# Norm sums taken tile by tile on groups of 32 of TensorE's columns, and the scaling of tiles reordered, in a four-layer transformer kernel on one core

## Chip, cores and metric

The kernel runs on one core of a Trainium2 chip, in one launch. The metric is the device time of that launch in microseconds (us). Each kernel is measured several times and the median is given. One further execution is recorded by the hardware profiler; all durations of single instructions come from it. For this program a change of the time by less than about 0.2% (6.3 us) can't be told from no change.

## What is computed

Two blocks of two layers each, on 512 tokens of 1024 features, in fp32 from end to end. Cut to what matters here:

```python
def rms_norm(x, gain):
    return x * lax.rsqrt(jnp.mean(x * x, axis=-1, keepdims=True) + EPS) * gain
# first block: layer 0 mixes with HGRN2 (8 heads of 128), layer 1 with sparse attention
for layer in range(2):
    h = h + mixer(rms_norm(h, attn_norm[layer]))     # inside HGRN2: one rms norm per head
    h = h + conv_ffn(rms_norm(h, ffn_norm[layer]))   # 1024 -> 2 x 2816 -> 1024
h = rms_norm(h, final_norm)
# second block: layer 0 mixes with rotary attention (q and k normed per head), layer 1 with Hyena
for i in range(2):
    x = x + g1 * mixer(rmsnorm(x, norm1_g[i]) * (1 + sc1) + sh1)
    x = x + g2 * conv_ffn_2(rmsnorm(x, norm2_g[i]) * (1 + sc2) + sh2)
return rmsnorm(x, final_g)
```

Nine norms of the whole residual are taken this way (two of them back to back between the blocks), and each is followed by a large matrix product that needs its result.

## The kernel before

The residual `x` stays in the chip's memory transposed: eight tiles `x[:, j, :]` of 128 features (partitions) by 512 tokens. A product is made exact enough by splitting both operands into a high part in fp32r and a low part, and by three passes (lines 515, 516, 517: high with high, high with low, low with high). A weight comes in items of up to 1 MB. SyncE loads them in their order through three raw buffers, ScalarE makes the high part (`split`, line 1130) and VectorE the low part (`split_low`, line 1615). `ahead(key)` on either engine means: after the work on item `key`, split the item three further on (`NW` = 3).

The program is written by hand as one list per engine, and the engines meet at named events: `mark` raises a semaphore, `at` gives what to wait for. Nothing reorders the lists. The stages are begin, hgrn, ffn0, dsa, ffn1, attn, ffn2, hy, ffn3 and the end.

A **handover** from one stage to the next runs as follows.

- TensorE, `residual`: four items (keys 0 to 3), each giving two tiles of the new residual through `project`, which goes through the eight feature tiles and for each makes three passes for the one and three for the other column half. `project` of the next stage needs a tile of normed input per step, six passes.
- VectorE, `residual` (lines 1673, 1675): adds the two new tiles to `x`, then `ahead(keys[n])`.
- ScalarE, `residual`: squares each new tile (`squares`, line 1167), then `ahead(keys[n])`. After the last key as well: the split for a later item stands behind the last two squares and ahead of what follows.
- GpSimd, `residual` (line 2261): adds squares 0 to 5 into one buffer `rb`.
- TensorE, `token_sums` (line 558): sums over partitions by matmuls whose moving operand is one column of ones: one set (four matmuls of 128x1, in two passes each, as all fp32 matmuls here) for the buffer of the six, one for square 6, one for square 7. The result is 128 tokens (partitions) by 4 columns.
- ScalarE, `rms` (line 1138): the root. VectorE, `inverse`: reciprocal (line 1629), then a copy of each column to 128 columns (line 1631). TensorE, `spread` (line 567): four matmuls against the identity bring the factors to 128 partitions by 512 tokens in bank `STAT`.
- `shifted`: for each of the eight tiles VectorE scales (line 1642), ScalarE takes the high part (line 1145, or 1148 with a shift, in modulated stages), VectorE makes the low part (line 1646 or 1648). VectorE's list is scale 0, low 0, scale 1, low 1, and so on:

```python
dve.scalar_tensor_tensor(t[:, :], x[:, j, :], gain(j), ps[STAT][:, :], MUL, MUL)
dve.wait_ge(*at("h", stage, j, "hi"))
m = dve.tensor_tensor(hl[:, j, :], t[:, :], high, SUB)
```

The second block's stages are modulated: `modulated` first makes the gains from the conditioning. Between the blocks `end_and_modulated` does two norms in one: it sums squares and squares times the squared gain, and computes the second factor from both. The end of the kernel norms and writes out.

The same parts serve three other places. `begin` transposes the input (line 616) and sums its squares. In hgrn each of eight heads is normed over its 128 features: one set of sums, root, reciprocal, copy, spread, while other heads' projections run. In attention twelve tiles of q and k, two heads each, are normed over 64 features: there `token_sums` has two columns (`pairs`) and `spread` is in `rotate_end`. Loads of weights for gates and of the second block's `ada_w` are issued on ScalarE's queue, all others on SyncE's.

## Time and profile before

| | |
|---|---|
| median of 3 executions | 3147.76 us (3147.2 to 3148.05) |
| profiled execution, its own time | 3144.56 us |
| span of the profiled execution | 3142.8 us |
| granted clock of TensorE, mean | 0.941 of 2.4 GHz |
| TensorE busy | 2874.8 us, 91% (13568 matmuls) |
| VectorE busy | 1794.6 us, 57% (2550) |
| ScalarE busy | 1017.5 us, 32% (1366) |
| GpSimd busy | 325.4 us, 10% (271) |

The span runs from the first to the last recorded instruction. The profiled execution's own time has a little around it, and the median of the other executions is 3.2 us above that. TensorE is busy nearly always, but a share is an average: what a change at a handover is worth is read from the order of events in it. In the timeline a matmul's duration overlaps the next one's start; the pitch from start to start is what it costs in a stream. The granted clock is TensorE's alone.

### The profile page before, as it was taken

How to read it: one execution, taken by the hardware profiler on the slowest of the kernel's cores; microseconds unless marked ns; L12 is line 12 of the kernel's file. 1: busy time of each engine (PE TensorE's matmuls, PEld its weight loads, DVE VectorE, ACT ScalarE, POOL GpSimd, SP SyncE). 2: the span in 40 equal slices, each digit the busy share in tenths (PEclk: the TensorE clock that was granted, in tenths of full speed). 3: DMA queues.
4: the chain of work that ended last, by engine and by line, in shares of the span. 5: the costliest groups of instructions: out<-in, count | busy, mean ns of one | idle time of the engine just before them, and what ended most of it. 6: DMA issues, size and time to landing. Idle time of an engine off the chain costs nothing.

```text
span 3142.8 us, 33865 instructions
## 1 busy us (share of the span) xinstructions
PE 2874.8 (91%) x13568; PEld 2308.3 (73%) x13568; DVE 1794.6 (57%) x2550; ACT 1017.5 (32%) x1366; POOL 325.4 (10%) x271
## 2 busy tenths in 40 slices
PE   7988789999997799999997789999998988899999
PEld 6777678888774478888783367888777777678887
DVE  3277746565576437474545536564655798554433
ACT  3223224242333434242424423232332233332322
POOL 0000000000001200000202310000000677200000
PEclk9999889999997899999898989999999688999999
DMA  5710114443322024343320015454421000322221
GB/s 141 154 41 27 41 54 144 134 133 112 89 67 68 21 77 141 121 141 97 102 67 14 1 54 163 155 174 133 140 81 44 26 18 22 111 78 94 95 86 47
DMA packets 260436, 275.67 MB, mean 88 GB/s; under 512 B 23159, under 2 KB 229495, under 8 KB 260280
## 3 DMA queue, kind: packets, MB, share of 16 engines
q1 hardware_dynamic: 230088, 218.44, 22.8%
q10 hardware_dynamic: 30192, 55.05, 5.6%
q8 instruction: 109, 1.79, 0.3%
q14 instruction: 47, 0.39, 0.0%
HBM read 266.13 MB, written 7.34 MB: 87 GB/s over the span
## 4 chain that ended last, share of the span: by engine, by line
PE 75%; DVE 14%; ACT 5%; issue 3%; DMA 1%; SPq 1%; POOL 0%; ACTq 0%; DVEq 0%; POOLq 0%
PE ps L515 21%; PE ps L517 21%; PE ps L516 21%; DVE sb L1615 2%; PE ps L800 2%; DVE sb L1642 2%; PE ps L665 1%; PE ps L558 1%; DMA sb<-in_hgrn_w_in 1%; PE ps L567 1%; PE ps L783 1%; PE ps L979 1%; ACT sb L1456 1%; DVE sb L2023 1%; DVE sb L2156 1%
## 5 line engine op out<-in xcount | busy, mean ns | idle before, releaser
L515 PE MATMUL ps<-sb 128*128 128x512 f32 (+1 forms) x3552 | 1364.6, 384 | 93.2 <-DVE sb L1648 18.8
L516 PE MATMUL ps<-sb 128*128 128x512 f32 (+1 forms) x3552 | 1347.4, 379 | 0.0
L517 PE MATMUL ps<-sb 128*128 128x512 f32 (+1 forms) x3552 | 1347.3, 379 | 0.0
L515 PEld LDWEIGHTS ps<-sb 128*128 128x128 f32 x3552 | 687.4, 194 | 248.6 <-issue 68.5
L517 PEld LDWEIGHTS ps<-sb 128*128 128x128 f32 x3552 | 687.1, 193 | 125.0
L516 PEld LDWEIGHTS ps<-sb 128*128 128x128 f32 x3552 | 688.1, 194 | 119.1 <-issue 0.7
L1615 DVE TENSOR_TENSOR sb<-sb 128x2048 fp32r<-128x2048 f32 (+2 forms) x198 | 446.6, 2256 | 372.2 <-ACT sb L1130 372.1
L1130 ACT ACTIVATE sb<-sb 128x2048 fp32r<-128x2048 f32 (+2 forms) x198 | 368.7, 1862 | 291.2 <-PE ps L517 272.5
L1800 DVE SCALAR_TENSOR_TENSOR sb<-ps,sb 128x511 f32<-128x511 f32 (+1 forms) x264 | 197.7, 749 | 190.2 <-ACT sb L1288 184.0
L2261 POOL TENSOR_TENSOR sb<-sb 128x512 f32<-128x512 f32 x45 | 62.1, 1387 | 1714.0 <-ACT sb L1167 1712.0
L1288 ACT ACTIVATE sb<-ps,sb 128x512 f32<-128x512 f32 x132 | 100.1, 774 | 304.9 <-PE ps L517 304.9
L783 PE MATMUL ps<-sb 128*128 128x128 f32 x416 | 75.7, 326 | 65.4 <-ACT sb L1342 62.2
L1675 DVE SCALAR_TENSOR_TENSOR sb<-ps,sb 128x512 f32<-128x512 f32 x64 | 46.3, 751 | 153.8 <-PE ps L517 153.6
L1820 DVE SCALAR_TENSOR_TENSOR sb<-sb 128x512 f32<-128x512 f32 x168 | 126.0, 750 | 12.9 <-DVE sb L1817 0.5
L783 PEld LDWEIGHTS ps<-sb 128*128 128x128 f32 x416 | 56.4, 167 | 102.7 <-issue 96.8
L2293 POOL TENSOR_SCALAR sb<-sb 128x512 f32<-128x512 f32 (+3 forms) x128 | 76.7, 612 | 485.7 <-DVE sb L1877 485.7
L1673 DVE TENSOR_TENSOR sb<-sb,ps 128x512 f32<-128x512 f32 x64 | 43.5, 687 | 127.4 <-PE ps L517 127.2
L1315 ACT ACTIVATE sb<-sb 128x512 fp32r<-128x512 f32 x88 | 55.3, 633 | 180.1 <-DVE sb L1842 108.5
L1167 ACT ACTIVATE sb<-sb 128x512 f32<-128x512 f32 x72 | 45.0, 642 | 206.0 <-DVE sb L1675 108.9
L1300 ACT ACTIVATE sb<-sb 128x512 f32<-128x512 f32 x88 | 55.6, 632 | 137.1 <-DVE sb L1800 137.1
L665 PEld LDWEIGHTS ps<-sb 128*128 128x128 f32 x512 | 72.6, 210 | 28.9 <-issue 23.6
L665 PE MATMUL ps<-sb 128*128 128x128 f32 x512 | 75.2, 295 | 18.8 <-DVE sb L1721 18.8
(213 smaller groups left out, 2354.2 us busy)
## 6 DMA issues: line engine op xcount, KB each, us to landing
sb<-in_ffn_w_up SPq DMA_DIRECT2D x88, 1024.0 KB, 5.1
sb<-in_ada_w ACTq DMA_DIRECT2D x192, 256.0 KB, 3.2
sb<-in_ffn_w_down SPq DMA_DIRECT2D x32, 1024.0 KB, 5.0
sb<-in_ffn_w_down SPq DMA_DIRECT2D x16, 768.0 KB, 4.3
sb<-in_hy_w_in SPq DMA_DIRECT2D x12, 1024.0 KB, 5.1
sb<-in_hgrn_w_in SPq DMA_DIRECT2D x8, 1024.0 KB, 11.1
sb<-in_hgrn_w_in SPq DMA_DIRECT2D x16, 512.0 KB, 5.5
sb<-in_dsa_w_in SPq DMA_DIRECT2D x6, 1024.0 KB, 5.3
```

The source lines that it names most:

```text
L515: pe.matmul(o, al, bh, start=f, stop=False, **kw)
L516: pe.matmul(o, ah, bl, start=False, stop=False, **kw)
L517: m = pe.matmul(o, ah, bh, start=False, stop=l, **kw)
L665: m = pe.matmul(ps[bk][:, c], a_[:, c], b_[:, c], start=True, stop=True)
L783: m = pe.transpose(ps[b][:, c], M.P[2 * (u % 4) + e][:, c], ident[:, :])
L800: m = pe.matmul(ps[b][64 * e:64 * e + 64, q0:L], value(j, s), M.PT[e][:, s, q0:L], start=s == 0, stop=s == 3, skip_group_check=True)
L1130: act.activation(wh[w][:, 0:n], raw[it["r"]][:, 0:n], ACTF.Copy).then_inc(*mark("act_hi", ("hi", it["key"])))
L1288: act.activation(dst[:, :], ps[b][:, :], ACTF.Identity, bias=bias(tile), scale=wt(offset, tile)).then_inc(*mark("act_ffn", (name + "_0", n ...
L1615: dve.tensor_tensor(wl[w][:, 0:n], raw[it["r"]][:, 0:n], wh[w][:, 0:n].bitcast(F), SUB).then_inc(*mark("dve_lo", ("lo", it["key"])))
L1800: dve.scalar_tensor_tensor(o, i, cv[0](tap, tile), o, MUL, ADD).then_inc(*mark("dve_ffn", (name, n, tile) if last else (name + "_1", n, ti ...
L1820: m = dve.scalar_tensor_tensor(a, w[:, :], cact[:, f:f + 1], a, MUL, ADD)
L2293: pool.tensor_scalar(P, P, M.rs[:, c:c + 1], 1.0, MUL, MUL).then_inc(*mark(f"pool_{stage}", ("scaled", stage, u, e)))
```

## The change

**Sums.** `sums` takes the place of `token_sums`. For each quarter `tt` of the tokens a matmul has 32 columns of ones as weights, the 128 columns of squares as the moving operand, and writes to partitions 32 tt to 32 tt + 31 of the bank: each quarter has its own group of 32 of TensorE's columns. The sum of a token thus stands on 32 partitions. Every tile of squares has its own set now: eight sets a norm (sixteen in the double norm, whose second kind goes to bank `OTHER`). Two sets stand behind key 1, two behind key 2, two between the column halves of key 3 (`project` has an argument `cols`), and two at the end. GpSimd's additions are gone.

**Factor.** `rms` and `inverse` work on 128 columns (256 in attention) in `rb`; the copy is gone; the double norm's steps are widened alike. `spread` multiplies, for each quarter, 32 partitions of the factor with ones: the 32 equal rows are summed, and `eps` and the scale carry 1024 to make up for it. Each of the four matmuls waits for the one before (`("spread", *name, tt - 1)`). `begin`, the heads and the rotary part use the same functions or the same form.

**Tiles.** VectorE's list in `shifted` is scale 0, scale 1, low 0, scale 2, low 1, and so on.

**Weights.** After the last key of a residual, `ahead` stands on ScalarE and VectorE no longer in `residual` but behind `shifted` of the next stage (argument `then`).

```diff
-STAT, OB, HB = 7, 3, 7
+STAT, OTHER, OB, HB = 7, 3, 3, 7
...
-    def project(sem, key, banks, done, then, tile=None, ready=None, rows=None):
+    def project(sem, key, banks, done, then, tile=None, ready=None, rows=None, cols=(0, 1)):
...
-    def token_sums(bank, src, cols, first, last, to=0):
-        n = cols.shape[1]
+    def sums(bank, squares, first, last):
         for tt in range(4):
-            m = pe.matmul(ps[bank][:, to + n * tt:to + n * tt + n], src[:, 128 * tt:128 * tt + 128], cols,
-                          start=first and tt == 0, stop=last, skip_group_check=True)
+            m = pe.matmul(ps[bank][32 * tt:32 * tt + 32, 0:128], ones[:, 0:32], squares[:, 128 * tt:128 * tt + 128],
+                          start=first, stop=last, skip_group_check=True)
         return m
-    def spread(bank, i, scaled, done):
-        pe.wait_ge(*at(*scaled))
-        wait_bank(bank)
+    def spread(bank, i, name):
+        pe.wait_ge(*at("inverse", *name))
         for tt in range(4):
-            m = pe.matmul(ps[bank][:, 128 * tt:128 * tt + 128], rb[i][:, 128 * tt:128 * tt + 128], ident[:, :],
-                          start=True, stop=True, skip_group_check=True)
-        m.then_inc(*mark("pe_stat", done))
+            p = slice(32 * tt, 32 * tt + 32)
+            if tt:
+                pe.wait_ge(*at("spread", *name, tt - 1))
+            pe.matmul(ps[bank][:, 128 * tt:128 * tt + 128], ones[p, :], rb[i][p, 0:128], start=True, stop=True,
+                      skip_group_check=True).then_inc(*mark("pe_stat", ("spread", *name, tt), *([("spread", *name)] if tt == 3 else [])))
     def normalise(stage, i):
-        freed[STAT] = [("rms", stage)]
-        spread(STAT, i, ("wide", stage), ("spread", stage))
+        spread(STAT, i, (stage,))
         freed[STAT] = [("t", stage, 7)]
     def residual(sem, r, keys, banks, ready, tile=None, stats=True, gain=False):
+        def squared(j):
+            for i in ((0, 1) if gain else (0,)):
+                if j == 0:
+                    wait_bank((STAT, OTHER)[i])
+                pe.wait_ge(*at("sq", r, i, j))
+                sums((STAT, OTHER)[i], (ht if i else sq)[j % 2], j == 0, j == NT - 1).then_inc(
+                    *mark("pe_stat", ("sq_used", r, i, j), *([("stat", r, i)] if j == NT - 1 else [])))
         for n in range(4):
-            bk = banks[n % 2]
-            project(sem, keys[n], bk, [("res", r, 2 * n + i) for i in range(2)],
-                    [[("x", r, 2 * n + i)] for i in range(2)], tile=tile, ready=ready)
+            names = [("res", r, 2 * n + i) for i in range(2)]
+            then = [[("x", r, 2 * n + i)] for i in range(2)]
+            if stats and n == 3:
+                project(sem, keys[n], banks[n % 2], names, then, tile=tile, ready=ready, cols=(0,))
+                squared(4)
+                squared(5)
+                project(sem, keys[n], banks[n % 2], names, then, tile=tile, ready=ready, cols=(1,))
+            else:
+                project(sem, keys[n], banks[n % 2], names, then, tile=tile, ready=ready)
+                if stats and n:
+                    squared(2 * n - 2)
+                    squared(2 * n - 1)
         if stats:
-            kinds = (0, 1) if gain else (0,)
-            for i in kinds:
-                if i == 0:
-                    wait_bank(STAT)
-                pe.wait_ge(*at("sum", r, i, 5))
-                token_sums(STAT, rb[i], ones[:, 0:1], i == 0, False, to=4 * i)
-                pe.wait_ge(*at("sq", r, i, 6))
-                token_sums(STAT, (ht if i else sq)[0], ones[:, 0:1], False, False, to=4 * i).then_inc(
-                    *mark("pe_stat", ("sq_used", r, i, 6)))
-            for i in kinds:
-                pe.wait_ge(*at("sq", r, i, 7))
-                token_sums(STAT, (ht if i else sq)[1], ones[:, 0:1], False, True, to=4 * i).then_inc(
-                    *mark("pe_stat", ("sq_used", r, i, 7), *([("stat", r)] if i == kinds[-1] else [])))
+            squared(6)
+            squared(7)
...
-            token_sums(b1, sq[n % 2], T.pairs[:, :], True, True).then_inc(*mark("pe_attn", ("rot_sum", n)))
-            freed[b1] = [("rms", "rot", n)]
+            for e in range(2):
+                for half in range(2):
+                    p = 64 * e + 32 * half
+                    m = pe.matmul(ps[b1][p:p + 32, 0:256], ones[64 * e:64 * e + 64, 0:32], sq[n % 2][64 * e:64 * e + 64, 256 * half:256 * half + 256],
+                                  start=True, stop=True, skip_group_check=True)
+            m.then_inc(*mark("pe_attn", ("rot_sum", n)))
...
         def rotate_end(n):
             b1 = ((4, 5), (6, 7))[n % 2][0]
-            spread(b1, n % 2, ("wide", "rot", n), ("spread", "rot", n))
+            pe.wait_ge(*at("inverse", "rot", n))
+            for half in range(2):
+                if half:
+                    pe.wait_ge(*at("spread", "rot", n, 0))
+                for e in range(2):
+                    p = slice(64 * e + 32 * half, 64 * e + 32 * half + 32)
+                    m = pe.matmul(ps[b1][64 * e:64 * e + 64, 256 * half:256 * half + 256], ones[p, 0:64], rb[n % 2][p, 0:256],
+                                  start=True, stop=True, skip_group_check=True)
+                m.then_inc(*mark("pe_stat", ("spread", "rot", n, half), *([("spread", "rot", n)] if half else [])))
...
-    def rms(i, heads, bank, n, done, name):
-        w = 4 * heads
+    def rms(i, bank, n, done, name, width=128):
         act.wait_ge(*at(*done))
-        act.activation(rc[i][:, 0:w], ps[bank][:, 0:w], ACTF.Sqrt, bias=eps[:, 0:1], scale=1.0 / n).then_inc(*mark("act_stat", name))
-    def shifted(stage, shift):
+        act.activation(rb[i][:, 0:width], ps[bank][:, 0:width], ACTF.Sqrt, bias=eps[:, 0:1], scale=1024.0 / n).then_inc(
+            *mark("act_stat", ("rms", *name)))
+    def shifted(stage, shift, then=None):
         for j in range(NT):
...
-    def normalise(stage, i, r, shift=None):
-        rms(i, 1, STAT, D, ("stat", r), ("rms", stage))
-        shifted(stage, shift)
+        if then:
+            ahead(then)
+    def normalise(stage, i, r, then, shift=None):
+        rms(i, STAT, D, ("stat", r, 0), (stage,))
+        shifted(stage, shift, then)
...
-            if j == 0:
-                dst = rb[i]
-            else:
-                dst = (ht if i else sq)[j % 2]
-                if j >= 3:
-                    act.wait_ge(*at("sum", r, i, j - 2))
+            dst = (ht if i else sq)[j % 2]
+            if j >= 2:
+                act.wait_ge(*at("sq_used", r, i, j - 2))
...
                 squares(r, 2 * n + 1, gain)
-            ahead(keys[n])
+            if n < 3 or not stats:
+                ahead(keys[n])
...
-    def inverse(i, heads, rooted, wide):
-        w = 4 * heads
-        dve.wait_ge(*at(*rooted))
-        dve.reciprocal(rc[i][:, 0:w], rc[i][:, 0:w]).then_inc(*step("inverse", wide))
-        dve.wait_ge(*at("inverse", wide))
-        dve.tensor_copy(rb[i][:, :].rearrange("p (c f) -> p c f", c=w),
-                        rc[i][:, 0:w].unsqueeze(2).broadcast_to([128, w, 128 // heads])).then_inc(*mark("dve_stat", wide))
-    def shifted(stage, r, gain, shift, within=None):
+    def inverse(i, name, width=128):
+        dve.wait_ge(*at("rms", *name))
+        dve.reciprocal(rb[i][:, 0:width], rb[i][:, 0:width]).then_inc(*mark("dve_stat", ("inverse", *name)))
+    def shifted(stage, r, gain, shift, then=None, within=None):
         dve.wait_ge(*at("spread", stage))
-        for j in range(NT):
-            t = ht[j % 2]
-            dve.wait_ge(*at("x", r, j))
-            if j >= 2:
-                dve.wait_ge(*at("h", stage, j - 2, "hi"))
-                dve.wait_ge(*at("h", stage, j - 2, "lo"))
-            dve.scalar_tensor_tensor(t[:, :], x[:, j, :], gain(j), ps[STAT][:, :], MUL, MUL).then_inc(*mark("dve_h", ("t", stage, j)))
-            dve.wait_ge(*at("h", stage, j, "hi"))
-            high = hh[:, j, :].bitcast(F)
-            if shift is None:
-                m = dve.tensor_tensor(hl[:, j, :], t[:, :], high, SUB)
-            else:
-                m = dve.scalar_tensor_tensor(hl[:, j, :], t[:, :], mod[:, shift + j:shift + j + 1], high, ADD, SUB)
-            m.then_inc(*mark("dve_h", ("h", stage, j, "lo")))
-            if j == 1 and within:
-                within()
-    def normalise(stage, i, r, gain, shift=None, within=None):
-        inverse(i, 1, ("rms", stage), ("wide", stage))
-        shifted(stage, r, gain, shift, within)
-    def modulated(stage, i, r, layer, gain, first):
+        for j in range(NT + 1):
+            if j < NT:
+                dve.wait_ge(*at("x", r, j))
+                if j >= 2:
+                    dve.wait_ge(*at("h", stage, j - 2, "lo"))
+                dve.scalar_tensor_tensor(ht[j % 2][:, :], x[:, j, :], gain(j), ps[STAT][:, :], MUL, MUL).then_inc(*mark("dve_h", ("t", stage, j)))
+            if j:
+                k = j - 1
+                dve.wait_ge(*at("h", stage, k, "hi"))
+                t, high = ht[k % 2], hh[:, k, :].bitcast(F)
+                if shift is None:
+                    m = dve.tensor_tensor(hl[:, k, :], t[:, :], high, SUB)
+                else:
+                    m = dve.scalar_tensor_tensor(hl[:, k, :], t[:, :], mod[:, shift + k:shift + k + 1], high, ADD, SUB)
+                m.then_inc(*mark("dve_h", ("h", stage, k, "lo")))
+                if k == 1 and within:
+                    within()
+        if then:
+            ahead(then)
+    def normalise(stage, i, r, gain, shift=None, then=None, within=None):
+        inverse(i, (stage,))
+        shifted(stage, r, gain, shift, then, within)
...
-            ahead(keys[n])
+            if n < 3 or not stats:
+                ahead(keys[n])
...
-    def residual(r, gain=False):
-        for j in range(1, NT - 2):
-            for i in ((0, 1) if gain else (0,)):
-                pool.wait_ge(*at("sq", r, i, j))
-                pool.wait_ge(*(at("sum", r, i, j - 1) if j > 1 else at("sq", r, i, 0)))
-                pool.tensor_tensor(rb[i][:, :], rb[i][:, :], (ht if i else sq)[j % 2][:, :], ADD).then_inc(
-                    *mark("pool_sum", ("sum", r, i, j)))
     def begin():
         pool.memset(ones[:, :], 1.0).then_inc(*mark("pool_begin", ("ones",)))
-        pool.memset(eps[:, :], EPS).then_inc(*mark("pool_begin", ("eps",)))
+        pool.memset(eps[:, :], 1024 * EPS).then_inc(*mark("pool_begin", ("eps",)))
...
-    normalise("ffn0", 1, 1, lambda j: v("ffn_norm", j))
+    normalise("ffn0", 1, 1, lambda j: v("ffn_norm", j), None, ("hgrn", "out", 3))
...
```

In the list of TensorE, at the end of the residual of hgrn and the start of ffn0's first product, there stood (behind the name of a semaphore is who is waited for: `act_sq` is ScalarE's squares, `act_stat` and `dve_stat` the factor's steps):

```order
L558 MATMUL ps<-sb 128x1 [waits pool_sum,dve_hgrn]
L558 MATMUL ps<-sb 128x1 x3
L558 MATMUL ps<-sb 128x1 [waits act_sq]
L558 MATMUL ps<-sb 128x1 x3
L558 MATMUL ps<-sb 128x1 [waits act_sq]
L558 MATMUL ps<-sb 128x1 x3
L567 MATMUL ps<-sb 128x128 [waits act_stat,dve_stat]
L567 MATMUL ps<-sb 128x128 x3
L515 MATMUL ps<-sb 128x512 [waits act_h,dve_h,dve_lo,act_hi]
```

and now stand:

```order
L514 MATMUL ps<-sb 128x512
L556 MATMUL ps<-sb 32x128 [waits act_sq]
L556 MATMUL ps<-sb 32x128 x3
L556 MATMUL ps<-sb 32x128 [waits act_sq]
L556 MATMUL ps<-sb 32x128 x3
L567 MATMUL ps<-sb 128x128 [waits dve_stat]
L567 MATMUL ps<-sb 128x128 [waits pe_stat] x3
L512 MATMUL ps<-sb 128x512 [waits act_h,dve_h,dve_lo,act_hi]
```

Two sets are left here instead of three, the other six stand in three pairs farther up among the products, and the spreading matmuls wait for each other.

In the list of VectorE, at the same place (`act_h` is the high part of a tile, `dve_x` the residual), there stood:

```order
L1673 TENSOR_TENSOR sb<-sb,ps 128x512 [waits pe_hgrn] x2
L1615 TENSOR_TENSOR sb<-sb 128x2048 [waits act_hi]
L1629 RECIPROCAL sb<-sb 128x4 [waits act_stat]
L1631 COPY sb<-sb 128x512 [waits dve_step]
L1642 SCALAR_TENSOR_TENSOR sb<-sb,ps 128x512 [waits dve_x,pe_stat]
L1646 TENSOR_TENSOR sb<-sb 128x512 [waits act_h]
L1642 SCALAR_TENSOR_TENSOR sb<-sb,ps 128x512 [waits dve_x]
L1646 TENSOR_TENSOR sb<-sb 128x512 [waits act_h]
L1642 SCALAR_TENSOR_TENSOR sb<-sb,ps 128x512 [waits dve_h,dve_x]
```

and now stand:

```order
L1685 TENSOR_TENSOR sb<-sb,ps 128x512 [waits pe_hgrn] x2
L1641 RECIPROCAL sb<-sb 128x128 [waits act_stat]
L1650 SCALAR_TENSOR_TENSOR sb<-sb,ps 128x512 [waits dve_x,pe_stat]
L1650 SCALAR_TENSOR_TENSOR sb<-sb,ps 128x512 [waits dve_x]
L1656 TENSOR_TENSOR sb<-sb 128x512 [waits act_h]
L1650 SCALAR_TENSOR_TENSOR sb<-sb,ps 128x512 [waits dve_h,dve_x]
L1656 TENSOR_TENSOR sb<-sb 128x512 [waits act_h]
L1650 SCALAR_TENSOR_TENSOR sb<-sb,ps 128x512 [waits dve_h,dve_x]
```

The weight's low part (128x2048) and the copy have left the way to the first scaling, and the second scaling has passed the first low part.

## Rows read from the trace of the kernel before

**Rows 1.** The chain of waits that ended last, share of the span by engine
```profile
PE 75%; DVE 14%; ACT 5%; issue 3%; DMA 1%; SPq 1%; POOL 0%; ACTq 0%; DVEq 0%; POOLq 0%
```
**Rows 2.** Timeline, TensorE, into ffn0: start, us, line, shape, count [idle before, releaser]
```profile
446.61 2.92 PE L558 MATMUL ps<-sb 128*128 128x1 f32 x24
452.89 2.07 PE L567 MATMUL ps<-sb 128*128 128x128 f32 x8 [3.36 <-DVE sb L1631]
457.29 0.77 PE L515 MATMUL ps<-sb 128*128 128x512 f32 x1 [2.32 <-DVE sb L1646]
...
471.63 0.47 PE L515 MATMUL ps<-sb 128*128 128x512 f32 x1 [0.42 <-DVE sb L1646]
```
**Rows 3.** The same view, VectorE
```profile
450.00 2.29 DVE L1615 TENSOR_TENSOR sb<-sb 128x2048 fp32r<-128x2048 f32 x1 [2.50 <-ACT sb L1130]
452.21 0.17 DVE L1629 RECIPROCAL sb<-sb 128x4 f32<-128x4 f32 x1
...
455.00 0.75 DVE L1642 SCALAR_TENSOR_TENSOR sb<-sb,ps 128x512 f32<-128x512 f32 x1 [2.17 <-PE ps L567]
456.45 0.69 DVE L1646 TENSOR_TENSOR sb<-sb 128x512 fp32r<-128x512 f32 x1 [0.70 <-ACT sb L1145]
457.06 0.74 DVE L1642 SCALAR_TENSOR_TENSOR sb<-sb,ps 128x512 f32<-128x512 f32 x1
```
**Rows 4.** The same view, ScalarE
```profile
446.85 1.32 ACT L1167 ACTIVATE sb<-sb 128x512 f32<-128x512 f32 x2 [7.76 <-DVE sb L1673]
448.07 1.89 ACT L1130 ACTIVATE sb<-sb 128x2048 fp32r<-128x2048 f32 x1
449.87 0.24 ACT L1138 ACTIVATE sb<-ps,sb 128x4 f32<-128x4 f32 x1
```
**Rows 5.** Windows: us, busy of PE, PEld, DVE, ACT, POOL, PEclk, DMA share, GB/s
```profile
450.00:453.00 3.00, 0.11 (x1) 0.11 (x1) 2.80 (x3) 0.12 (x1) 0.00 (x0) 0.50 0.00 0
463.00:466.00 3.00, 3.00 (x14) 2.33 (x13) 2.30 (x4) 0.63 (x1) 0.00 (x0) 1.00 0.01 3
```
**Rows 6.** Timeline, TensorE in attention: two groups of 64 columns, and rows halved
```profile
1733.86 0.65 PE L800 MATMUL ps<-sb 128*64 128x512 f32 x2
...
1734.34 0.60 PE L800 MATMUL ps<-sb 128*64 128x512 f32 x2
...
998.26 0.49 PE L868 MATMUL ps<-sb 64*128 64x128 f32 x4
998.68 0.44 PE L873 MATMUL ps<-sb 128*128 128x128 f32 x2
```
**Rows 7.** Timeline, TensorE in hgrn: sums and spread of a head
```profile
283.87 0.95 PE L558 MATMUL ps<-sb 128*128 128x1 f32 x8
...
265.12 1.06 PE L567 MATMUL ps<-sb 128*128 128x128 f32 x8
```
**Rows 8.** Groups by line and form, VectorE: count, busy us, mean ns, idle before
```profile
L1877 DVE RECIPROCAL sb<-sb 128x2 f32<-128x2 f32 x64 | 10.5, 164 | 71.1 <-ACT sb L1456 39.6 <-ACT sb L1405 31.5
...
L1629 DVE RECIPROCAL sb<-sb 128x8 f32<-128x8 f32 x12 | 2.4, 200 | 9.7 <-ACT sb L1138 9.7
```
**Rows 9.** Timeline, TensorE, spread of the norm into dsa
```profile
834.07 1.26 PE L567 MATMUL ps<-sb 128*128 128x128 f32 x8 [0.82 <-DVE sb L1631]
```
**Rows 10.** Timeline, VectorE, scalings of a modulated norm (into attention)
```profile
1543.35 0.74 DVE L1642 SCALAR_TENSOR_TENSOR sb<-sb,ps 128x512 f32<-128x512 f32 x1
...
1545.55 0.74 DVE L1642 SCALAR_TENSOR_TENSOR sb<-sb,ps 128x512 f32<-128x512 f32 x1
```
**Rows 11.** The chain in order of time, first 135 us: start, us, what
```profile
27.19 3.33 PE ps L558 x16
...
33.65 0.76 DVE sb L1642
...
53.43 2.30 DVE sb L1615
...
77.27 39.04 DMA sb<-in_hgrn_w_in
```

More of the change, by code:

```diff
@@ L1578, in act_program @@
             hgrn()
[L1579 removed]
+            normalise("ffn0", 1, 1, ("hgrn", "out", 3))
             ffn(0, "hgrn")
[L1581 removed]
+            normalise("dsa", 0, 4, ("ffn0", "down", len(GROUPS) - 1, 3))
             dsa("ffn0")
[L1583 removed]
+            normalise("ffn1", 1, 5, ("dsa", "out", 3))
             ffn(1, "dsa")
@@ L1658, in modulated @@
+            def normalise(stage, i, r, gain, shift=None, then=None, within=None):
+                inverse(i, (stage,))
+                shifted(stage, r, gain, shift, then, within)
+            def modulated(stage, i, r, layer, gain, first, then):
                 base = 48 * layer + 8 * first
```

122 lines of the change are left out of this document (52 added, 70 removed).

## The prediction

> **What bounds the kernel now.** I read the chain of waits first, then the engines one by one over one handover, then single forms. The chain [rows 1] is 75% TensorE and 14% VectorE: TensorE sets the end, and other engines count where it waits for them. The places that this change touches are the handovers: a stage's last product is done, the norm of the residual is made, and the next stage's first projection starts. I follow the one into ffn0. TensorE's dense work ends at about 446.6, and it starts its sums there [rows 2]. ScalarE has the last square at 446.85 + 1.32 = 448.17, spends 448.07 to 449.96 on the high part of a weight that is due two projections later, and only then takes the root at 449.87 [rows 4]. VectorE makes that weight's low part from 450.00 to 452.29, then the reciprocal and the copy until TensorE can spread at 452.89 [rows 2, 3]. The first scaled tile starts at 455.00. From there tiles come every 457.06 - 455.00 = 2.06 us [rows 3], because VectorE scales a tile, waits for ScalarE's high part, subtracts, and only then scales the next. TensorE needs six passes a tile, 1.40 us at 14 passes in 3.00 us and rounding up to 0.23 each [rows 5]. So it waits at each tile, and its last tile starts at 471.63 [rows 2]; with its six passes that projection ends at 473.0. In the pause the granted clock is 0.50, that is 1.2 GHz, and it is 1.00 (2.4 GHz) again at 463 [rows 5].
>
> **The pause, part by part (into ffn0).** Unchanged up to the last square, 448.17.
> The sums: four fp32 matmuls, two passes each, of 128 columns on four column groups. The trace has none with four groups. The nearest are those with two groups of 64 columns: two passes start within the same 0.01 us at 1733.86, the next two at 1734.34, for 512 columns [rows 6], so groups run side by side. A set of 128 columns is then 2 x 0.11 = 0.22 us of stream, and alone, with weights and drain, about 0.45. Bounds: 0.3, and the 0.95 that a set costs today [rows 7]. I take 0.45, nearer to the tiled rows because it is the same mechanism. Today the last set ends near 449.5; now 448.6.
> The root over 128 columns instead of 4: 0.24 now [rows 4], I take 0.35; 449.0. It no longer stands behind the high part.
> The reciprocal over 128 columns: 2 columns take 164 ns and 8 take 200 [rows 8]: 6 ns a column, so 0.164 + 126 x 0.006 = 0.92 us, against 0.68 from the start of today's reciprocal to the spread, with the copy [rows 2, 3]. Bounds 0.3 and 1.2. Done at 450.0, with semaphores. The low part's 2.29 is gone from here.
> The Trainium skill, "VectorE: DVE Perf Modes", section "First, the fixed hardware budget", has the reciprocal repeat its divide eight times; at the 0.96 GHz that the page gives, an estimate for 128 columns is 1.2 us with the fixed part. By that the sum below would be some 4 us worse. The rows bear out six cycles, not eight, and decide.
> The spread: four matmuls that now each wait for the one before. One alone, from weights to result, is 0.49 us at the high clock: the four passes at 998.26 are two matmuls side by side [rows 6]. With a semaphore's trip that is 0.55 each, 2.2 us; at the low clock, where eight passes take 2.07 against 1.06 [rows 2, 7], some 0.85 each, 3.4. Bounds 1.1 and 4.0. The clock will have fallen in most handovers; I take 3.0. First scaled tile: 453.05, not 455.00. Gain 1.95.
> The tiles: scaling now runs one ahead. VectorE's own work bounds them: 0.75 + 0.69 less the overlap of 0.07, 1.37 a tile [rows 3], shorter than TensorE's 1.40. So TensorE, which starts 2.3 us after the first scaling as now, is bound by itself: 453.05 + 2.3 + 8 x 1.40, and 2.3 for the first 3.7 to 5.7 us at half clock, which the waits hid before: 468.9 against 473.0. Gain over the handover: 4.15 us.
>
> **What is paid inside the residual projections.** Eight sets per norm instead of three; six of them (j = 0 to 5) stand in the middle of the dense stream, in three pairs. A pair is 4 x 0.11 = 0.44 of stream plus the way into tiling and out. The two row-tiled matmuls at 998.26 hold TensorE 0.42 until 998.68 for 0.22 of stream [rows 6], so 0.2 a switch there and back, and I add 0.1 for weights not loaded ahead: 0.75 a pair, 2.25 a norm. Bounds for a pair 0.5 and 1.8 (as today's sets). The Trainium skill, "TensorEngine Tiling (Array Packing)", section "Key Properties", says that changing the tiling mode drains the engine, which speaks against this placing; by that rule, the trace agrees, at the 0.2 just read.
> The three sets of today lie behind the last product, and two of them are hidden by the last square; GpSimd's additions are off the path too. Both cost nothing when they go. Splitting the last key by columns brings x6 forward by half a projection, hidden under the other half. The moved parts of weights come 12 us into the first projection; their weight is due 22 us or more after its start, so they are hidden there, behind the last tile, on engines that then wait for that projection's end. SyncE's load of the third weight after it starts as much later, and has most of two projections to spare, and ffn0's load issues on ScalarE's queue follow the moved high part; ScalarE is then at most 0.5 us late for the first gate, which frees a bank that is wanted 20 us later.
>
> **The sum over the kernel.**
> - ffn0, ffn1: 4.15 - 2.25 = 1.9 each, 3.8.
> - ffn2, hy, ffn3 (modulated): tiles came every 1545.55 - 1543.35 = 2.20 us [rows 10], 1.45 now, so 0.95 more; two small VectorE operations also leave the path, 0.45: 3.4 each, 10.
> - dsa: the moved weight has 136 columns, so about 1.1 less leaves the path, and its spread ran at the high clock, 1.26 at 834.07 [rows 9], where mine costs 2.3 or more, 1.8 less again: 1 us worse.
> - attention's: double squares, six pairs of sets doubled (3.9), wide factors for both norms, two spreads before the first product: 0.
> - last norm: nothing to move away and no tile order; spread and reciprocal +0.7, sets +2.25: 3 worse.
> - eight heads in hgrn: sums 0.95 to 0.45, root +0.05, reciprocal +0.3 (the copy ran under its successor), spread from 1.06 to 2.2 [rows 7]; both lie on the way TensorE to VectorE and back: 1.0 worse each, 8.
> - rotary, 12 tiles: spread in two waiting halves +0.35 each, sums on four groups -0.2, and the last pair with 256-wide reciprocals (0.16 + 254 x 0.006 = 1.7 us) some 1 late; 2.6 worse.
> - begin: the chain runs through two sets of sums of 3.33 at 27.19 (half clock), the first scaling at 33.65, a weight's low part at 53.43 to 55.73, and SyncE's queue behind it to a load that lands at 116 [rows 11]. Sets of about 0.75 for 1.5 let squares and sums end 4 us sooner, VectorE's low part of the first weight then holds the reciprocal at 26.2, first scaling 30.6: 3.0. Six tiles run ahead of that low part at 1.37 for 2.06, and two before it: 4.6. All that follows moves with it: 7.6 better.
> Together 3.8 + 10 - 1 + 0 - 3 - 8 - 2.6 + 7.6 = 6.8 us better. The profiled execution took 3144.6 us (span 3142.8), 3.2 below the median of the three runs, 3147.8; so 3137.8 there, and as a median **3141 us**. About 6.3 us (0.2%) is what a measurement of this kernel tells from no change.
>
> **Rivals.**
> A, the forecast: 3131 to 3149, mostly over the 0.2% line. Chance 0.48 (0.36 faster, 0.12 same).
> B, the serial spread takes it back. Each of four steps costs 1.1 us, at low clock with a slow way through the semaphore: 4.4 a spread, 1.4 more in eight handovers and 1.6 more in eight heads less what the clock gives, about +10 us: 3151, no change. For it: no row shows a matmul waiting on the one before. Against: 0.49 for one alone. Chance 0.17 (0.15 same).
> C, slower: four column groups run one after another, so a set in the stream costs 0.9 as now, a pair 1.8. There are 27 pairs, so 27 x 1.05 = +28 us: 3169. It turns the sign from 1.0 us a pair on. Against it: two groups do overlap. The Trainium skill, "TensorE: Matmul & The Clock Gate", "Part 3: Packing small matmuls — row/col tiling", measures a gain from three column groups; by that, C is unlikely. Chance 0.13.
> D, the clock stays high, since the pause is shorter and has work in it: spread 2.2 for 3.0 and 2.3 of slow start gone, 3 us in five handovers: 3126. Against: the clock fell to 0.50 by 450 [rows 5]. Chance 0.15.
> E, the scaling ahead does not do what it says: the next scaling waits for the low part before it, and if that wait costs 0.5 us a tile stays near 2 us. Seven handovers give 2.3 less, begin 4: +20, 3161. Chance 0.07.
> Faster 0.36 + 0.15 = 0.51; same 0.12 + 0.15 + 0.02 = 0.29; slower 0.02 + 0.13 + 0.05 = 0.20. The range reaches over A, B, most of D and E's edge, and leaves out most of C: 3124 to 3158.
>
> **What would show it.** Right: no idle time of TensorE at single tiles of a first projection; first scaling 6.4 us after the last dense pass in ffn0, not 8.4; sums of four groups starting together and a pair holding the stream for about 0.75; reciprocals of 128 columns near 0.9; the begin's third low part done at 48 instead of 55.7; each head 1 us longer. Wrong: a pair over 1.1, spreads over 4, or tiles still 2 us apart; or a new wait of TensorE for the moved weight part.

## The result, and the profile after

| | before | changed |
|---|---|---|
| median of 20 executions each, side by side | 3150.36 us | 3154.2 us (3150.75 to 3161.49) |
| ratio to before, 95% interval | | 1.0017 (1.001 to 1.0025) |
| profiled execution, its own time | 3144.56 us | 3151.13 us |
| span | 3142.8 us | 3149.3 us |
| TensorE busy, matmuls | 2874.8 us, 13568 | 2867.8 us, 13928 |
| granted clock, mean | 0.941 | 0.941 |

The changed kernel is 0.17% slower, about 5.4 us; the forecast was 6.8 us faster. The time lies in the range of 3124 to 3158, but on the other side of the kernel before. The interval leaves out 1, so the sign is clear, though the size is below the 0.2% named above.

The handover into ffn0 went as the prediction has it, and gained more (5.6 us for 4.15). Timeline of the changed kernel, TensorE (columns as in [rows 2]): the last dense pass started at 443.37.

```profile
443.69 0.42 PE L556 MATMUL ps<-sb 128*32 128x128 f32 x8
445.19 0.43 PE L556 MATMUL ps<-sb 128*32 128x128 f32 x8 [1.08 <-ACT sb L1180]
447.10 2.49 PE L567 MATMUL ps<-sb 32*128 32x128 f32 x8 [1.48 <-DVE sb L1641]
451.90 0.77 PE L512 MATMUL ps<-sb 128*128 128x512 f32 x1 [2.32 <-DVE sb L1656]
```

The same stretch on VectorE and on ScalarE:

```profile
446.09 0.95 DVE L1641 RECIPROCAL sb<-sb 128x128 f32<-128x128 f32 x1 [1.61 <-ACT sb L1151]
449.62 1.41 DVE L1650 SCALAR_TENSOR_TENSOR sb<-sb,ps 128x512 f32<-128x512 f32 x2 [2.58 <-PE ps L567]
451.06 0.69 DVE L1656 TENSOR_TENSOR sb<-sb 128x512 fp32r<-128x512 f32 x1
451.86 0.75 DVE L1650 SCALAR_TENSOR_TENSOR sb<-sb,ps 128x512 f32<-128x512 f32 x1
...
453.31 0.75 DVE L1650 SCALAR_TENSOR_TENSOR sb<-sb,ps 128x512 f32<-128x512 f32 x1
```
```profile
444.51 0.63 ACT L1180 ACTIVATE sb<-sb 128x512 f32<-128x512 f32 x1 [5.65 <-DVE sb L1685]
445.69 0.37 ACT L1151 ACTIVATE sb<-ps,sb 128x128 f32<-128x128 f32 x1 [0.55 <-PE ps L556]
```

A set of sums takes 0.42 (0.45 was taken), the root 0.37 (0.35), the reciprocal of 128 columns 0.95 (0.92), the spread 2.49 (3.0, bounds 1.1 and 4.0). Scalings come every 1.45 us instead of 2.06 [rows 3], with the first two back to back. TensorE has no idle time at single tiles here. The first scaling starts 6.25 us after the start of the last dense pass, 6.0 after its end by pitch (6.4 forecast).

One place is new. The handover into attention, TensorE of the changed kernel:

```profile
1527.21 1.05 PE L735 MATMUL ps<-sb 128*128 128x1 f32 x8
1532.27 5.92 PE L567 MATMUL ps<-sb 32*128 32x128 f32 x16 [4.01 <-DVE sb L1979]
1556.71 0.77 PE L512 MATMUL ps<-sb 128*128 128x512 f32 x1 [18.52 <-issue]
```

and VectorE (line 1984 is the scaling by the factor of the final norm, the last user of what TensorE spread from 1535.2 on):

```profile
1546.27 1.62 DVE L1658 SCALAR_TENSOR_TENSOR sb<-sb 128x512 fp32r<-128x512 f32 x2
1548.94 2.29 DVE L1628 TENSOR_TENSOR sb<-sb 128x2048 fp32r<-128x2048 f32 x1 [1.05 <-ACT sb L1143]
1551.15 5.35 DVE L1984 SCALAR_TENSOR_TENSOR sb<-sb,ps 128x512 f32<-128x512 f32 x8
```

TensorE waits 18.52 us before the first product of attention. The profile names no releaser ("issue"), but the wait ends 0.2 us after the last of the eight final scalings, at 1556.50. Before, that product started at 1543.58, 2.4 us behind the first scaling, and the final scalings ran beside it.

The two traces side by side, stage by stage. The dense passes are the same 10656 in both; I take the start of the last one before a norm and of the 48th behind it (eight tiles), and give by how much the changed kernel is ahead. The change of that lead is what a piece gained:

| piece | lead at its end, us | gain | forecast |
|---|---|---|---|
| begin, with the weight loads behind it (to pass 120) | 10.9 | +10.9 | +7.6 |
| heads of hgrn | 6.7 | -4.2 | -8 |
| residual of hgrn (three pairs of sets) | 3.0 | -3.7 | -2.25 |
| handover into ffn0 | 8.6 | +5.6 | +4.15 |
| ffn0 | 5.9 | -2.7 | -2.25 |
| handover into dsa | 7.1 | +1.2 | +1.25 |
| dsa | 1.5 | -5.6 | -2.25 |
| handover into ffn1 | 7.1 | +5.6 | +4.15 |
| ffn1 (double norm's sets) | 3.1 | -4.0 | -3.9 |
| **handover into attention** | -9.4 | **-12.5** | **+3.9** |
| attention | -15.2 | -5.8 | -4.85 |
| handovers into ffn2, hy, ffn3 | | +5.8, +4.6, +6.8 | +5.65 each |
| ffn2, hy | | -2.7, -3.9 | -2.25 each |
| ffn3 and the last norm | -6.5 | -1.9 | -3 |

All rows but one are within 4 us of the forecast, and together they miss by 3 us. The handover into attention misses by 16.4 us, more than the whole gap of 13.3 us between the forecast and these two traces.

One trace of each kernel doesn't fix every row. The eight heads (from pass 120 to pass 960) take 337.5 us before and 341.7 in the changed kernel, but 346.9 in the trace of e2 and 349.9 in that of e4 (experiments below), whose heads are the same code as the changed kernel's. In the same way hy takes 3.7 us longer in e3's trace than before, with unchanged code. The row of the handover into attention stands far above such differences; those of the heads and of hy don't.

### The profile page after: what moved, and what is told of

Same layout as the page of the kernel before. It is cut to its first block, busy times and chain, and to the rows that moved or that the text cites. A ratio compares the mean times of both kernels' runs of the same rounds, so it can differ in the third digit from the quotient of the medians.

```text
span 3149.3 us, 34446 instructions
## 1 busy us (share of the span) xinstructions
PE 2867.8 (91%) x13928; PEld 2253.1 (72%) x13928; DVE 1811.0 (58%) x2520; ACT 1019.4 (32%) x1366; POOL 263.2 (8%) x226
## 4 chain that ended last, share of the span: by engine, by line
PE 78%; DVE 13%; ACT 3%; issue 3%; DMA 1%; SPq 1%; POOL 0%; ACTq 0%; DVEq 0%; POOLq 0%
PE ps L512 22%; PE ps L514 22%; PE ps L513 22%; PE ps L803 2%; DVE sb L1628 1%; PE ps L669 1%; PE ps L786 1%; PE ps L567 1%; DMA sb<-in_hgrn_w_in 1%; PE ps L993 1%; ACT sb L1469 1%; DVE sb L2165 1%; DVE sb L2032 1%; PE ps L871 1%; PE ps L556 1%
## 5 line engine op out<-in xcount | busy, mean ns | idle before, releaser
L669 PEld LDWEIGHTS ps<-sb 128*128 128x128 f32 x512 | 68.4, 199 | 31.8 <-issue 26.6
L2262 POOL TENSOR_TENSOR sb<-sb 128x1024 fp32r<-128x1024 f32 (+1 forms) x33 | 87.1, 2652 | 31.8 <-ACT sb L1527 17.5
```

The lines of the kernel that those rows point to most:

```text
L669: m = pe.matmul(ps[bk][:, c], a_[:, c], b_[:, c], start=True, stop=True)
L2262: pool.tensor_tensor(dst, src, high.bitcast(F), SUB).then_inc(*mark(sem, (*name, "lo")))
```

## Experiments

Each was measured four to six times beside the kernel before on the same chip; the ratio is to before, and 0.001 is 3.15 us. My theory after the two traces: the product waits for bank 3. `OTHER` = 3 holds the second factor now (it was bank 6), `freed[OTHER] = [("x", 9, 7)]` sets its release at the last final scaling, and the first product of attention is `project(..., (0, 1) if g else (2, 3), ...)`, banks 2 and 3.

**e1_bank6**

```diff
-                spread(OTHER, 0, ("final",))
-                freed[OTHER] = [("x", 9, 7)]
+                freed[OTHER] = []
+                wait_bank(6)
+                spread(6, 0, ("final",))
+                freed[6] = [("x", 9, 7)]
```

> The changed kernel, with the factor of the final norm spread into bank 6, as before, in place of bank 3. Theory 1 (bank): the first product of attention is written to banks 2 and 3 and waits until the last of eight final scalings has read bank 3. Then that product starts about 2.4 us after the first scaling instead of 21.1, and the kernel is 16 to 18 us faster than the changed one: a ratio to before of 0.996 to 0.9965. Theory 2 (moved weight): the product waits for a weight whose parts were moved behind the scaling. Then nothing changes, ratio 1.0017.

**e2_attn_weight_back**: `ahead(keys[3])` of ffn1's residual stands in the residual again, on both engines.

> The changed kernel, with the high and low part of ffn1's last weight made ahead of the norm again, into attention alone; bank 3 as in the change. Theory 1 (bank): the final scalings end 3.2 us sooner but the norm starts 2.1 us later: 1 us faster than the changed kernel at most, ratio 1.0014 to 1.0020, and the first product still starts right behind the last final scaling. Theory 2 (moved weight): the wait of 18.5 us is gone, ratio about 0.9965.

Measured: e1 0.9958 (0.9945 to 0.997), e2 1.0028 (1.0016 to 1.004). TensorE in e1:

```profile
1533.41 5.92 PE L567 MATMUL ps<-sb 32*128 32x128 f32 x16 [4.01 <-DVE sb L1981]
1539.26 0.80 PE L512 MATMUL ps<-sb 128*128 128x512 f32 x1
```

and in e2, where the final scalings ran from 1557.94:

```profile
1542.41 5.92 PE L567 MATMUL ps<-sb 32*128 32x128 f32 x16 [6.54 <-DVE sb L1979]
1563.50 0.76 PE L512 MATMUL ps<-sb 128*128 128x512 f32 x1 [15.18 <-issue]
```

With bank 6 the product starts 2.5 us behind the first scaling (1536.78), and 19 us come back. Without the moved weight the product still starts right behind the final scalings (1557.94 + 5.35 = 1563.29). So it is the bank. The median of e2 lies above its forecast of 1.0014 to 1.0020, but its interval overlaps that. The handover doesn't explain the difference: up to the 48th pass it takes 0.2 us less in e2's trace than in the changed kernel's, since the first scaling comes 2.5 us later and the product 3.4 us sooner behind it. The trace as a whole is 8.6 us longer, 5.3 of them in the heads, where the code is the same.

**e3_tiles_alone** and **e4_tiles_back**: only the loop of VectorE's `shifted` changes places between the kernels.

```diff
-                for j in range(NT):
-                    ...
-                    dve.scalar_tensor_tensor(t[:, :], x[:, j, :], gain(j), ps[STAT][:, :], MUL, MUL)
-                    dve.wait_ge(*at("h", stage, j, "hi"))
-                    ...
+                for j in range(NT + 1):
+                    if j < NT:
+                        ...
+                    if j:
+                        k = j - 1
+                        dve.wait_ge(*at("h", stage, k, "hi"))
+                        ...
```

> The kernel before, with VectorE's scaling one tile ahead of the low parts and nothing else. By the two traces, first scaling to 48th pass takes 17.9 us before and 14.6 in the changed kernel (19.1 and 15.2 in modulated norms). Theory 1: the whole difference belongs to the order of tiles, 3.3 in three norms, 3.9 in four, 4 to 5 at the begin: 29 us faster, ratio 0.9905 to 0.992. Rival: part of the pitch is made up for by the first slow passes and by later waits: 12 us, ratio 0.996.

> The changed kernel, with VectorE's order of tiles as before and nothing else. Theory 1: slower than the changed kernel by about 28 us (3.3 in three norms, 3.9 in three, 5.5 into attention, where the final scalings stand behind the tiles, and 4 to 5 at the begin), ratio to before 1.0095 to 1.011. Rival: 12 us, ratio 1.0055.

Measured: e3 0.9911 (0.9898 to 0.9925), e4 1.0118 (1.0104 to 1.0132). Both ways agree: 28 us off the kernel before, as expected, and 32 us onto the changed one, a little over the expected range. VectorE in e3, into ffn0; the first scaling stands at the same distance from the last dense pass as before (8.63 us), and only the pitch is new:

```profile
452.50 1.41 DVE L1641 SCALAR_TENSOR_TENSOR sb<-sb,ps 128x512 f32<-128x512 f32 x2 [2.17 <-PE ps L567]
...
454.74 0.75 DVE L1641 SCALAR_TENSOR_TENSOR sb<-sb,ps 128x512 f32<-128x512 f32 x1
...
456.19 0.75 DVE L1641 SCALAR_TENSOR_TENSOR sb<-sb,ps 128x512 f32<-128x512 f32 x1
```

So one part of the change alone is 28 us faster, and the rest, even with the bank mended, gives 15 of them back on balance (e1 against e3). The next runs look for what is in these 15.

**e5_one_mode_spread**: as e1, and the spread over all rows. `fans` is 128 x 4: column `tt` is one on partitions 32 tt to 32 tt + 31, else zero.

```diff
-                    p = slice(32 * tt, 32 * tt + 32)
-                    if tt:
-                        pe.wait_ge(*at("spread", *name, tt - 1))
-                    pe.matmul(ps[bank][:, 128 * tt:128 * tt + 128], ones[p, :], rb[i][p, 0:128], ...)
+                    m = pe.matmul(ps[bank][:, c], fans[:, tt:tt + 1].broadcast_to([128, 128]), rb[i][:, 0:128], ...)
```

> e1_bank6, with the factor spread by four matmuls over all 128 rows, against columns that are one in one group of 32 rows and zero elsewhere, so that none waits for the one before and the mode doesn't change. Attention's rotary part as in the change. Theory (the serial spread costs): such a set takes 1.1 us at the high clock and 2.1 at the low one, as before the change, in place of 2.3 and 2.5 to 3.4: 0.4 to 1.3 us in eight norms, 2.1 into attention, and up to 1 in each of eight heads, 8 to 14 us in all, ratio 0.9915 to 0.9935. Rival: in the heads it is hidden behind other heads' work, and 5 us at most come back, ratio 0.9943.

**e12_one_mode_waits**: e5 with the wait for the matmul before put back.

> e5_one_mode_spread with one thing of the change back: each of the four spreading matmuls waits for the one before; they stay at all 128 rows. It tells the waits from the rows. Theory (the waits cost): a set takes 2.1 us at the high clock as in e1_bank6, and most of the 24 us between e5 (0.9883) and e1 (0.9958) are lost again, ratio 0.994 to 0.996. Rival (the groups of 32 rows and their change of mode cost): a set takes 1.2 us, ratio 0.988 to 0.9895.

Measured: e5 0.9883 (0.9868 to 0.9898), e12 0.9932 (0.9918 to 0.9947). The group of the spread by line and form, of e1, of e12 and of e5:

```profile
L567 PE MATMUL ps<-sb 32*128 32x128 f32 x144 | 42.9, 392 | 21.0 <-DVE sb L1643 13.8 <-DVE sb L1981 4.0
```
```profile
L569 PE MATMUL ps<-sb 128*128 128x128 f32 x144 | 44.8, 405 | 20.9 <-DVE sb L1645 13.8 <-DVE sb L1983 4.0
```
```profile
L567 PE MATMUL ps<-sb 128*128 128x128 f32 x144 | 26.1, 342 | 17.8 <-DVE sb L1643 13.8 <-DVE sb L1981 4.0
```

A spread in a head takes 2.11 us in e1, 2.02 in e12 and 1.06 in e5. Such a set with the dense pass behind it, of e1, of e12 and of e5:

```profile
225.68 2.11 PE L567 MATMUL ps<-sb 32*128 32x128 f32 x8
227.72 0.50 PE L512 MATMUL ps<-sb 128*128 128x512 f32 x1
```
```profile
223.56 2.02 PE L569 MATMUL ps<-sb 128*128 128x128 f32 x8
225.34 0.48 PE L513 MATMUL ps<-sb 128*128 128x512 f32 x1
```
```profile
223.02 1.06 PE L567 MATMUL ps<-sb 128*128 128x128 f32 x8
223.83 0.48 PE L513 MATMUL ps<-sb 128*128 128x512 f32 x1
```

The waits are the greater part: nearly all of a set's own time, and 0.0049 of the 0.0075 between e1 and e5, 15 us. The other 0.0026, 8 us (by the widths of the intervals 0.0007 to 0.0045), goes with the groups of 32 rows, and the rows bear it out. From the start of the matmul ahead of the set to the second dense pass behind it, a set in a head costs 2.58 us in e1, 2.21 in e12 and 1.24 in e5: 0.97 by the waits and 0.37 by the groups. Neither run came out in its expected range: e5 gained more than the 0.9915 to 0.9935, and e12 lost less of it again than the 0.994 to 0.996.

**e6_tiles_and_weight**: e3 with `ahead(keys[3])` behind `shifted` on both engines, as in the change.

> The kernel before with two parts of the change, the order of tiles and the weight's parts behind the scaling; sums and factor as before. Theory: the root no longer stands behind a high part nor the reciprocal behind a low part, 2.2 us less in five norms, 0.8 into dsa, nothing into attention (TensorE's own sums are last there): 12 us faster than e3_tiles_alone, ratio 0.987 to 0.988. Rival: the moved parts delay a later product by as much, ratio 0.991.

Measured: 0.9845 (0.983 to 0.986), 21 us better than e3, where 12 were expected. Into ffn0 the root and reciprocal of e6 follow the sums at once (in the kernel before they stood behind 1.89 and 2.29 us of weight work [rows 3, 4]):

```profile
442.50 3.22 PE L558 MATMUL ps<-sb 128*128 128x1 f32 x24
442.73 1.32 ACT L1169 ACTIVATE sb<-sb 128x512 f32<-128x512 f32 x2 [7.76 <-DVE sb L1679]
445.75 0.26 ACT L1138 ACTIVATE sb<-ps,sb 128x4 f32<-128x4 f32 x1 [1.70 <-PE ps L558]
446.05 0.18 DVE L1632 RECIPROCAL sb<-sb 128x4 f32<-128x4 f32 x1 [2.66 <-ACT sb L1138]
```

From last dense pass to first scaling: 8.63 to 6.59 in ffn0, 8.63 to 5.84 in ffn1, 9.10 to 6.37, 9.34 to 7.53 and 9.10 to 5.71 in the modulated three, 6.91 to 7.17 in dsa. That is 12.5 us in all, as expected; the traces' leads add to 15 us, and the interval of the difference between the two ratios (14 to 27 us) reaches down to there. What the rest of the 21 us is, if it is there, stays open.

**e7_sums_at_end** and **e8_both**: GpSimd adds squares 0 to 5 again, and three sets on column groups stand behind the last product, whose last key isn't split by columns; in e7 on e1, in e8 on e5.

```diff
-                squared(4)
-                squared(5)
-                project(sem, keys[n], banks[n % 2], names, then, tile=tile, ready=ready, cols=(1,))
-                ...
+                pe.wait_ge(*at("sum", r, i, 5))
+                sums(bank[i], rb[i], True, False)
+                pe.wait_ge(*at("sq", r, i, 6))
+                sums(bank[i], (ht if i else sq)[0], False, False)
```

> e1_bank6, with squares 0 to 5 of a residual added by GpSimd as before and three sets of sums on column groups behind the last product, and no split of the last key by columns. Theory (sums inside the stream cost): three pairs of 0.84 us a norm go, 1.6 more for the double norm, 24 us; the second-to-last square comes later, 0.7 us in each pause, 6 us: 16 to 18 us faster than e1_bank6, ratio 0.9902 to 0.991. Rival: GpSimd's sum is late or the three sets take the place of the pairs: no gain, 0.9958.

> e7_sums_at_end and e5_one_mode_spread together. Theory: both gains add, ratio 0.986 to 0.988. Rival: one hides behind the other, 0.990.

Measured: e7 0.9889 (0.9874 to 0.9903), 22 us better than e1; e8 0.9808 (0.9795 to 0.9822), 3091.83 us against 3151.67. Both are below their expected ranges, and the two gains add: e5's 24 us and e7's 22 off e1 give 0.9814. The pairs inside the stream cost what they were thought to cost. A pair in the changed kernel's trace, between two dense passes that would be 0.23 us apart:

```profile
430.81 0.39 PE L514 MATMUL ps<-sb 128*128 128x512 f32 x1
431.12 0.65 PE L556 MATMUL ps<-sb 128*32 128x128 f32 x16
431.70 0.50 PE L512 MATMUL ps<-sb 128*128 128x512 f32 x1
432.04 0.40 PE L513 MATMUL ps<-sb 128*128 128x512 f32 x1
```

0.89 for 0.23, and 0.34 for the next 0.23: 0.77, and by the lead of the two traces around single pairs 0.76 to 0.80; the 0.84 of the expectation was a little too much. 27 of them are 21 us. At the end two of the three sets hide under the squares, and the third follows the last square at once (e8, ScalarE and TensorE; the last dense pass started at 435.15):

```profile
435.47 0.42 PE L557 MATMUL ps<-sb 128*32 128x128 f32 x8
435.62 1.31 ACT L1177 ACTIVATE sb<-sb 128x512 f32<-128x512 f32 x2 [7.76 <-DVE sb L1682]
436.30 0.42 PE L557 MATMUL ps<-sb 128*32 128x128 f32 x8 [0.41 <-ACT sb L1177]
436.98 0.43 PE L557 MATMUL ps<-sb 128*32 128x128 f32 x8 [0.25 <-ACT sb L1177]
437.48 0.37 ACT L1145 ACTIVATE sb<-ps,sb 128x128 f32<-128x128 f32 x1 [0.55 <-PE ps L557]
```

The 0.7 us that I expected to lose in each pause aren't there as a rule: the first scaling into ffn0 comes 4.93 us behind the last dense pass, in e5 5.73. Over seven handovers this distance changes by -0.9 to +0.6 us from e5 to e8, -1.2 in all; from e1 to e7 it is +0.8 in all.

**e9_rotary_one_mode** has the rotary factors by `fans` too, **e10_last_key_split** splits the last key by columns in e8, **e11_both_of_these** both.

> e8_both, with attention's rotary factors spread over all 128 rows too, in four matmuls on two column groups and no wait between the halves. Two tiles' spread takes 2.14 us in the changed kernel and 1.95 before. Theory: a turn's pair takes 1.1 us, 6 x 1 = 6 us less at most, of which the turns hide a part: 2 to 5 us, ratio 0.9793 to 0.9802. Rival: the turns are bound by other engines, 0.9808.

> e8_both, with the last key of each residual taken column half by column half, as in the change, so that square 6 is made under the last product. Theory: the pause is one square shorter (0.65 us) in eight norms, two squares into attention, 5 to 6 us, ratio 0.979 to 0.9793. Rival: the sum of six on GpSimd or its set of sums comes last then, no gain.

> e9 and e10 together, the fastest version that the runs so far suggest: ratio 0.977 to 0.979 if the two add, 0.9795 if only one holds.

Measured: 0.9815 (0.9799 to 0.9832), 0.9818 (0.9805 to 0.9832), 0.981 (0.9797 to 0.9824): nothing beyond e8, and both theories fail. In e9 there was little to gain: the 96 matmuls (with both passes) of the rotary spread keep TensorE busy for 12.1 us, against 13.0 in e8, where 6 us less were expected. In e10 the first scaling into ffn0 stands 4.92 us behind the last dense pass, in e8 4.93. The last square ends 1.77 us behind the start of that pass in e10 (433.83 to 435.60) and 1.78 in e8 (435.15 to 436.93): in a joint product the first half ends three passes ahead of the second, so square 6 is done by the time that tile 7 is added, split or not. My expectation for e10 had overlooked that. e8 remains the fastest.

## Why the prediction failed, by its own steps

**Attention's handover at 0: wrong, and this alone turns the sign.** That term names sets, factors and two spreads, and gives no reason why they come to 0 beyond the 3.9 for the sets. It says nothing of what the first product waits for, which leaves its start behind the second scaling as before. The change of `OTHER` from 6 to 3 was not followed to the next user of bank 3. The wait costs 18.6 us (e1 against the changed kernel, 0.0059). Without it the changed kernel stands at 0.9958, 13 us under the kernel before where 6.8 were forecast: the right sign, at twice the size. None of the five rivals was this one, and that the time still lies in the range is luck: the range was drawn for other rivals. The list of what would prove the forecast wrong had "a new wait of TensorE for the moved weight part": a new wait at that place it was, but e2 shows that the weight has no share in it.

**Sums: right.** 0.42 us for 0.45. Eight passes of 128 columns take no longer than that, and rival C, that groups run one after another, falls: a set in the stream holds less than half of the 0.95 that a set of before takes [rows 7], and a pair costs 0.77 for the 0.75 that was taken. e7 confirms the stage losses of some 2.4 each. The 6 ns a column that I read from the rows for the reciprocal hold as well: 0.95 us for 128 columns. The estimate from "VectorE: DVE Perf Modes" in the Trainium skill, section "First, the fixed hardware budget", would be 1.2; here the measurement decides. The page "TensorE: Matmul & The Clock Gate", section "Part 3: Packing small matmuls — row/col tiling", of the Trainium skill agrees, in that packed column groups gain.

**Spread: right, and its size is what the rival B asked about.** 2.11 us at the high clock (2.2 taken), 2.1 to 3.3 in the handovers (3.0 taken). B wanted 4.4; its terms (1.4 in eight handovers, 1.6 in eight heads) add to 24 us, and no reading stands behind the 10 that it makes of them "less what the clock gives". What the sum hid is how much could be had at this place: the price of the waits is 15 us (e12 against e5).

**Tiles: right in kind, too small in size.** A pitch of 1.37 was forecast; it is 1.45, or 1.36 a tile with the first two back to back. The tile order gives 28 us (e3); my handover terms and the begin have some 20 of it. (For the modulated norms 3.4 was written where the terms give 1.9 + 0.95 + 0.45 = 3.3.) Part of the rest is the clock. In the handover into ffn0 the windows, columns as in [rows 5], show it fall later behind the last dense pass and to the same level. First the kernel before, 2.6 to 5.6 us after the start of that pass, then the changed kernel at the same distance and right behind it:

```profile
449.00:452.00 3.00, 0.53 (x5) 0.44 (x4) 2.00 (x1) 1.11 (x2) 0.00 (x0) 0.55 0.00 0
```
```profile
446.00:449.00 3.00, 1.73 (x7) 1.09 (x8) 0.95 (x1) 0.06 (x1) 0.00 (x0) 0.91 0.00 0
449.00:452.00 3.00, 0.68 (x3) 0.41 (x3) 2.24 (x4) 1.26 (x2) 0.00 (x0) 0.50 0.00 0
```

I added 2.3 us of slow passes to every handover. In this one they end sooner: passes take 0.63 us until 455.02 and 0.39 from 455.39 on, 3.5 us behind the first dense pass at 451.90, which costs 1.7 us; before, that took from 457.29 to 462.96, 5.7 us. A shorter pause doesn't always end so: in e8, whose pause into ffn0 is shorter still, the slow passes last from 442.36 to 448.46, 6.1 us.

**Weight behind the scaling: right.** Hidden where it went (ffn0 and ffn1 take the same time in e6 as in e3), 1.8 to 3.4 us in five pauses.

**Heads at -8: not contradicted.** The two traces give 4.2 us for eight, but the same heads cost 4.9 us in e1's trace, 9.5 in e2's and 12.4 in e4's, each against the kernel before. The spread did grow by 1.05 us (2.11 for [rows 7]'s 1.06). From the spread of one head to that of the next, the first five steps take 30.7 us each before; in the changed kernel they take 30.2 or 31.8, and in e2 once 33.5. The last two, where less other work is left to fill the waits, went from 25.6 and 14.9 to 26.5 and 16.3.

**Begin at +7.6: too small.** The load that landed at 116.3 [rows 11] now lands at 105.4. The first scaling starts at 28.47, not at the 30.6 forecast, because the first weight's low part is done at 23.7 and the reciprocal starts at 24.1, not at 26.2. From there to the third low part (done at 45.5, forecast 48) the gain is 5.0 us for 4.6. The chain of the changed kernel in order of time:

```profile
46.86 19.08 SPq L2365
66.03 39.40 DMA sb<-in_hgrn_w_in
```

**dsa at -2.25: 3.3 us more are lost.** Some of it is at its end. The last product of values, 16 matmuls, runs at half clock in the changed kernel and at full clock in the kernel before; the windows over it:

```profile
1092.00:1096.00 4.00, 3.26 (x10) 1.38 (x12) 0.59 (x1) 0.00 (x0) 0.00 (x0) 0.50 0.00 0
```
```profile
1098.00:1101.00 3.00, 2.12 (x16) 1.23 (x16) 0.69 (x1) 0.00 (x0) 0.00 (x0) 1.00 0.02 5
```

It takes 4.46 us instead of 2.38. e1 and e6 have it at half clock too (4.54), e3 not (2.38). That looks like the moved weight, but e9 has the moved weight and runs these matmuls in 2.38 us, at a granted clock of 1.00. So the cause stays open, and with it what the rest of the 3.3 us is.

**The chances.** D, that the clock stays up through the pause, is seen in part in e8: its spread into ffn0 runs at the high clock and takes 1.16 us. But the clock falls just behind it, and the slow passes that D wanted gone are there:

```profile
438.50:441.50 3.00, 1.16 (x8) 0.97 (x8) 1.73 (x3) 0.63 (x1) 0.00 (x0) 1.00 0.00 0
441.70:444.70 3.00, 2.34 (x6) 1.89 (x7) 2.79 (x5) 1.23 (x3) 0.00 (x0) 0.50 0.00 0
```

The changed kernel, with its longer pause, shows neither. E, that the tiles don't run ahead, falls with e3: the wait that it names is there, but a scaling starts 0.1 us behind the end of the low part before it (at 451.86, behind 451.06 + 0.69), not 0.5. B falls with the spread's times.

## What to carry to other kernels

When a change gives a buffer or a bank another number, list the next writer of the new one and the last reader before it, as one does for a wait. An idle time that the profile puts down to "issue" is best explained by what ended just ahead of it on the other engines. And take a change of several parts apart before judging it: here one part was worth 28 us and another 21, while a bank number cost 19, sums in the stream 22 and waits between four small matmuls 15; together (28 + 21 - 19 - 22 - 15 = -7, measured -5) they read as hardly any change. The parts were measured on different kernels, and the smaller ones (wider root and reciprocal, rotary) not at all, so that the sum comes out near is a check and no proof.

## What the runs showed of the hardware

Four matmuls on four groups of 32 columns, in two passes each over 128 columns, take 0.42 to 0.43 us (443.69 and 445.19 in the changed kernel). A pair of such sets in the dense stream costs 0.77 us. A matmul of 128 columns (two passes) that waits for the one before costs 0.5 us at the high clock (2.02 us for four in e12), against 0.27 in a row (1.06 in e5). A stationary operand that is one column read 128 times works and costs no more than a full one (1.06 us a set in e5, 1.06 before). How long the clock stays low after a pause does not follow from the pause alone: into ffn0 the slow passes last 5.7 us before, 3.5 in the changed kernel and 6.1 in e8, with the first scaling 8.6, 6.2 and 4.9 us behind the last dense pass.
